# Grouped-query attention: the two heads of a query tile handled as a pair in every step

## The chip, the cores and the metric

One core of a Trainium2 chip. The metric is the device time of one execution in microseconds (us); smaller is better. TensorE is written PE, VectorE DVE, ScalarE ACT, GpSimdE POOL, SyncE SP.

## The reference, cut to what matters

Two different transformer blocks of two layers each, 512 tokens, model width 1024, all in float32. The first block runs four mixers side by side in each of its layers: a Fourier mix, grouped-query attention (GQA), an mLSTM scan and differential attention, then a feed-forward part. The change touches only the GQA, which runs twice, once in each layer of the first block:

```
q = apply_rope(rms_norm(q, g0)); k = apply_rope(rms_norm(k, g1))     # 8 query heads, 2 key heads, 64 wide
sc = einsum('blkgd,bskd->bkgls', q, k) * scale                        # per head 512 x 512
p  = softmax(sc, axis=-1)
y  = einsum('bkgls,bskd->blkgd', p, v)
```

## The kernel before

Activations lie transposed: features on the 128 partitions, 512 tokens along the free axis. Every large product (projections, gates, branch products, feed-forward) goes through one **stream**. One stream step is one call of `next(going)` in `steps` (L497 to L518): three fp32r matmuls of 128x128 by 128x512, high and low halves of weight and input (L508, L509, L510). `advance(n)` issues n steps. Most products are 8 steps long, a branch product is 4 (two of them share a weight unit). Weights come in pieces of 4 steps: SP loads `raw`, ACT rounds it to `wh` (L969), POOL takes the difference `wl` (L2035), in a ring of 4 pieces.

What is not a stream product is woven into the stream by hand. `tensor_program`, `scalar_program` and `vector_program` hold the same loops, and `beat(i, ...)` tells ACT and DVE how many products and pieces PE has issued at that place, so that each engine evicts finished products (DVE, `leave` L1376 and others; `branch_out` L1451), applies tanh or squares (ACT) and splits pieces (`split_weights`, which at a beat waits for the piece that PE finished there, L967 to L969) at the same place in its own order. All engines work strictly in the order written.

**GQA stage** (L679 to L714). A task is one head and one block of 128 queries: 32 tasks, ordered query tile p, head, block j. The two heads of a tile lie on partitions 0 to 63 and 64 to 127. For task t:

- PE `scores` (L566): one float32 matmul, 64 rows deep, 128x512 result, in bank 2, 3 or 4 by t % 3.
- DVE `maximum` (L1583), ACT `soften` (L1113, exponential straight from the bank, with the sum), DVE `normalise` (L1613 reciprocal, L1618 scaling), the latter in step t+1.
- PE `turn_over` (L575): four 128x128 transposes in bank 5 or 6 by t % 2, in step t+3. ACT `keep_turned` (L1131) copies them to `probT`.
- After block 3, in step t+4, PE multiplies with the values (L707): four matmuls 128 deep with 64 columns of weights, each 512 columns wide, out on partitions 0 to 63 of bank 7 for the first head, 64 to 127 for the second. After the second head ACT and DVE split bank 7 into the high and low halves of a branch input (L1000, L1385).

Step t is: scores(t), `advance(2)`, turn_over(t-3), the value products where due, `advance(2)`; n+5 = 37 steps, 148 stream steps. The query tiles 2 and 3 are still being prepared inside the loop: `mean` (L540) and `turn_rope` (L546) on PE, `rstd` on ACT (L975 loads the table of logarithms, L983 Ln, L985 Exp), `normed`, `straight` and `turned` on DVE. Their banks are 6 (tile 2) and 5 (tile 3), the banks of the transposes, and `take(b, ...)` makes PE wait until the last reader of a bank is done.

**The stream during and after the GQA** (`stream1`, L113). Counted in steps from the stage's first score, products end at: gate 8, bq 2 at 16, branch 20 and 24, bq 3 at 32, gates 40 and 48, branch 52 and 56, gates 64 and 72, branch 76 and 80, gates 88 and 96, branch 100 and 104, then cq 112, ck 120, cv 128, co 136, cq 144, gate 152, ck 160, gate 168, cv 176, branch 180 and 184, co (tile 1) 192, cq 200, gate 208, ck 216, gate 224, cv 232, branch 236 and 240, co (tile 2) 248, cq 256, gate 264, ck 272, gate 280, cv 288, branch 292 and 296, co (tile 3) 304, and so on to dq 1 at 360, dk 1 at 368.

**The mLSTM stage** follows (L717 to L764): four heads, each with `turn_values` (L554), four small matmuls (L727, L731) into banks 4 to 7, `advance(6)`, and nine scan steps of `advance(3)`, `advance(2)`, so 51 stream steps a head. At the end of head h ACT copies the four result banks out (`sums_of`, L1218 and L1219), and the next head's L727 waits for it. In the ninth scan step of head h, DVE first evicts what has ended in `advance(3)` and then runs `output_low` (L1385) for head h-1, and `sums_of(h)` waits for that. After the four heads: `advance(4)`, `turn_values`, `finish_of(i, "dk", 1)`, which runs the stream up to the end of dk 1, wherever it stands.

The differential attention later uses the same `scores` with two score matmuls a task, one on partitions 0 to 63 and one on 64 to 127, next to each other in the order.

Of the kernel before, what the change touches and what calls it, by code (L numbers as in the profile page):

```python
# [15 lines left out]
P = 128  # L16
# [236 lines left out]
class Program:  # L253
# [75 lines left out]
    def gqa_tasks(self):  # L329
        out = []  # L330
        for p in range(4):
            for hd in range(2):
                rows = slice(hd * HQ, (hd + 1) * HQ)
                probT = self.w(8, 4) if hd == 0 else self.w(17, 4)
                for j in range(NT):
                    out.append(Task([self.gqa_q(p)[rows, :]], [self.w(23)[rows, :]], j, S, 0, probT, 2 * p + hd,
                                    j == NT - 1, slot=hd))
        return out
# [121 lines left out]
def tensor_program(g):  # L460
# [117 lines left out]
    def layer1(i):  # L578
# [101 lines left out]
        n = len(tasks)  # L680
        probs = [w(4 + r) for r in range(4)]
        for t in range(n + 5):
            if t == 0:
                pe.wait_ge(s_dve, at("V", "rope", i, "k"))
            if t < n:
                if t % 8 == 0:
                    pe.wait_ge(s_dve, at("V", "rope", i, f"q{t // 8}"))
                scores(i, "gqa", tasks, t)
            if t == 1:
                turn_rope(i, chains["q1"])  # L690
            if t in (8, 14):
                mean(i, chains["q2" if t == 8 else "q3"])
            if t in (11, 17):
                turn_rope(i, chains["q2" if t == 11 else "q3"])
            advance(2)
            beat(i, "gqa", t, 0)
            if 0 <= t - 3 < n:
                turn_over(i, "gqa", tasks, t - 3, probs[(t - 3) % 4])
            if 0 <= t - 4 < n and tasks[t - 4].last:
                k = tasks[t - 4]  # L700
                hd = k.slot
                pe.wait_ge(s_act, at("C", "pT", i, "gqa", t - 4))
                if hd == 0:
                    pe.wait_ge(s_dve, at("V", "vt", i, "gqa"))
                    take(7, s_dve, "V", "H", i, 1, k.head // 2)
                for m in range(NT):
                    mm = nc.tensor.matmul(bank[7][hd * HQ:(hd + 1) * HQ, :],  # L707
                                          w(24)[:, m * P + hd * HQ:m * P + (hd + 1) * HQ],
                                          k.probT[:, m * S:(m + 1) * S], start=m == 0, stop=m == NT - 1)
                mm.then_inc(s_pe, T("pv", i, "gqa", k.head))  # L710
            advance(2)
            beat(i, "gqa", t, 1)
# [241 lines left out]
def scalar_program(g):  # L954
# [178 lines left out]
    def layer1(i):  # L1133
# [43 lines left out]
        n = len(tasks)  # L1177
        probs = [[w(4 + r) for r in range(4)]]
        for t in range(n + 5):
            if t < n:  # L1180
                soften(i, "gqa", tasks, t, probs)
            beat(i, "gqa", t, 0)
            if t in (8, 14):
                name = "q2" if t == 8 else "q3"
                rstd(i, name, g.gqa_chain(i, name).bank, g.gqa_chain(i, name).tmp)
            if 0 <= t - 3 < n:
                keep_turned(i, "gqa", tasks, t - 3)
            if 0 <= t - 4 < n and tasks[t - 4].last and tasks[t - 4].slot == 1:
                head = tasks[t - 4].head
                act.wait_ge(s_pe, at("T", "pv", i, "gqa", head))  # L1190
                branch_high(i, 1, head // 2, bank[7][:, :])
            beat(i, "gqa", t, 1)
# [159 lines left out]
def vector_program(g):  # L1352
# [396 lines left out]
    def layer1(i):  # L1749
# [80 lines left out]
        n = len(tasks)  # L1830
        probs = [[w(4 + r) for r in range(4)]]
        for t in range(n + 5):
            if t < n:
                maximum(i, "gqa", tasks, t, probs)
            beat(i, "gqa", t, 0)
            if t in (1, 11, 17):
# [618 lines left out]
```

## Time and profile before

| what | value |
|---|---|
| median of 3 runs | 3653.83 us (3651.8 to 3656.82) |
| profiled execution: its own time | 3656.83 us |
| profiled execution: span, first to last instruction | 3655.5 us |
| mean granted PE clock over the span | 0.981 |
| GQA stage, layer 0 and layer 1 | 192.3 us each |

The profile is of one execution. PE is its matmuls, PEld its weight loads. Matmuls overlap their neighbours in the records, so the price of an instruction is read from start to start, not from its own length. A float32 matmul shows as two records. Idle time before a group, and what ended it, stands in brackets.

### The profile page before, as it was taken

What the parts mean: (1) busy time and instruction counts of PE and PEld (TensorE: products, weight loads), DVE (VectorE), ACT (ScalarE), POOL (GpSimd) and SP (SyncE); (2) the same over time, 40 slices, a digit from 0 to 9 for tenths busy, and PEclk for the clock granted to TensorE, in tenths of its full rate; (3) what the DMA queues carried; (4) which work ended last, traced back from release to release, by engine and by line L of the source; (5) the groups of instructions that cost most, each with busy time, mean ns of one, the idle gap of its engine ahead of it and who ended that gap; (6) DMA issues with size and microseconds to landing.
All of it is one profiled execution on the core that took longest, in us unless ns stands there. A gap on an engine that the chain in (4) does not pass through costs nothing.

```text
span 3655.5 us, 39205 instructions
## 1 busy us (share of the span) xinstructions
PE 3515.7 (96%) x14412; PEld 2601.9 (71%) x14412; DVE 1459.8 (40%) x2796; ACT 1367.3 (37%) x2605; POOL 1320.1 (36%) x1016
## 2 busy tenths in 40 slices
PE   8999999999999999999999989988899999789999
PEld 5556776787787755667677778864588886468887
DVE  3432457444324243255644352355422124542212
ACT  2343334533223244333544322345433234543222
POOL 1222333344444322323244534430144443025444
PEclk9999999999999999999999999998999999899999
DMA  4111112233323211112123322210033322013333
GB/s 159 52 67 55 58 64 65 69 98 122 99 95 96 64 52 47 63 55 70 58 77 111 111 81 94 97 64 24 31 110 104 97 95 81 12 41 104 98 98 104
DMA packets 154751, 286.80 MB, mean 78 GB/s; under 512 B 17980, under 2 KB 20061, under 8 KB 154432
## 3 DMA queue, kind: packets, MB, share of 16 engines
q1 hardware_dynamic: 153232, 281.90, 23.9%
q8 instruction: 115, 1.88, 0.2%
q10 hardware_dynamic: 1328, 2.39, 0.2%
q14 instruction: 76, 0.62, 0.1%
HBM read 278.85 MB, written 5.37 MB: 78 GB/s over the span
## 4 chain that ended last, share of the span: by engine, by line
PE 83%; DVE 9%; ACT 5%; issue 2%; POOL 2%; DMA 0%; ACTq 0%; POOLq 0%; DVEq 0%
PE bank L508 23%; PE bank L510 22%; PE bank L509 22%; PE bank L566 3%; DVE work L1425 2%; POOL wl L2035 2%; PE bank L707 2%; PE bank L625 2%; PE bank L575 1%; ACT wh L969 1%; DVE work L1376 1%; PE bank L742 1%; PE bank L756 1%; PE bank L754 1%; PE bank L933 1%
## 5 line engine op out<-in xcount | busy, mean ns | idle before, releaser
L2035 POOL TENSOR_TENSOR wl<-raw,wh 128x512 fp32r<-128x512 f32 x1012 | 1319.9, 1317 | 2323.7 <-ACT wh L969 2100.0
L508 PE MATMUL bank<-Uh,wh 128*128 128x512 f32 x2720 | 1144.4, 421 | 36.5 <-POOL wl L2035 22.3
L510 PE MATMUL bank<-Uh,wl 128*128 128x512 f32 x2720 | 1068.9, 393 | 0.0
L509 PE MATMUL bank<-Ul,wh 128*128 128x512 f32 x2720 | 1067.5, 392 | 0.0
L969 ACT ACTIVATE wh<-raw 128x512 fp32r<-128x512 f32 x1012 | 601.8, 621 | 641.3 <-PE bank L510 621.3
L508 PEld LDWEIGHTS bank<-Uh,wh 128*128 128x128 f32 x2720 | 515.1, 189 | 255.0 <-issue 117.6
L509 PEld LDWEIGHTS bank<-Ul,wh 128*128 128x128 f32 x2720 | 516.3, 190 | 123.0 <-issue 23.0
L510 PEld LDWEIGHTS bank<-Uh,wl 128*128 128x128 f32 x2720 | 514.6, 189 | 112.0
L1376 DVE TENSOR_TENSOR work<-bank,rs 128x512 f32<-128x512 f32 x308 | 212.8, 691 | 895.1 <-PE bank L510 857.8
L508 PE MATMUL bank<-Hh,wh 128*128 128x512 f32 x1258 | 503.1, 400 | 9.0 <-ACT work L1060 5.9
L510 PE MATMUL bank<-Hh,wl 128*128 128x512 f32 x1258 | 490.4, 390 | 0.0
L509 PE MATMUL bank<-Hl,wh 128*128 128x512 f32 x1258 | 490.1, 390 | 0.0
L508 PEld LDWEIGHTS bank<-Hh,wh 128*128 128x128 f32 x1258 | 236.1, 188 | 84.4 <-issue 12.1
L510 PEld LDWEIGHTS bank<-Hh,wl 128*128 128x128 f32 x1258 | 236.1, 188 | 50.3
L509 PEld LDWEIGHTS bank<-Hl,wh 128*128 128x128 f32 x1258 | 236.4, 188 | 48.3 <-issue 1.9
L1410 DVE TENSOR_TENSOR xT<-xT,bank 128x512 f32<-128x512 f32 x128 | 88.0, 688 | 437.8 <-PE bank L510 437.8
L1075 ACT ACTIVATE work<-work 128x512 f32<-128x512 f32 x88 | 55.7, 633 | 380.6 <-DVE work L1425 245.8
L1081 ACT ACTIVATE Hh<-work 128x512 fp32r<-128x512 f32 x88 | 55.8, 634 | 312.4 <-DVE work L1437 312.4
L566 PE MATMUL bank<-work 64*128 64x512 f32 (+4 forms) x352 | 143.7, 592 | 4.1 <-DVE small L1587 4.1
L1113 ACT ACTIVATE work<-work,small 128x512 f32<-128x512 f32 (+3 forms) x160 | 95.5, 597 | 124.6 <-DVE small L1597 85.0
L1015 ACT ACTIVATE work<-xT 128x512 f32<-128x512 f32 x72 | 45.4, 630 | 204.8 <-DVE xT L1410 188.5
L575 PEld LDWEIGHTS bank<-const,work 128*128 128x128 f32 x588 | 75.0, 143 | 59.4 <-issue 17.8
(206 smaller groups left out, 2841.5 us busy)
## 6 DMA issues: line engine op xcount, KB each, us to landing
raw<-in_units SPq DMA_DIRECT2D x1012, 256.0 KB, 2.8
work<-in_dft SPq DMA_DIRECT2D x6, 512.0 KB, 9.4
xT<-in_xT SPq DMA_DIRECT2D x8, 256.0 KB, 9.2
scratch<-work SPq DMA_DIRECT2D x1, 2048.0 KB, 7.7
out<-xT SPq DMA_DIRECT2D x8, 256.0 KB, 2.9
table<-scratch SPq DMA_DIRECT2D x4, 448.0 KB, 5.1
work<-in_dft SPq DMA_DIRECT2D x2, 640.0 KB, 11.3
scratch<-table SPq DMA_DIRECT2D x1, 1152.0 KB, 5.3
```

The source lines that it names most:

```text
L508: nc.tensor.matmul(out, H, xh, start=k == 0, stop=False)
L509: nc.tensor.matmul(out, H, xl, start=False, stop=False)
L510: mm = nc.tensor.matmul(out, L, xh, start=False, stop=k == x.kt - 1)
L566: nc.tensor.matmul(bank[b][:, 0:k.nk], q[:, k.j * P:(k.j + 1) * P], keys[:, k.key0:k.key0 + k.nk], start=True, stop=True).then_inc(s_pe, T ...
L575: mm = nc.tensor.transpose(bank[b][:, n * P:(n + 1) * P], prob[:, n * P:(n + 1) * P], c("ident"))
L625: mm = nc.tensor.matmul(bank[b][:, :], g.work[:, x:x + P], w(8 + 4 * cs + j), start=j == 0 and cs == 0, stop=j == NT - 1 and cs == 1)
L707: mm = nc.tensor.matmul(bank[7][hd * HQ:(hd + 1) * HQ, :], w(24)[:, m * P + hd * HQ:m * P + (hd + 1) * HQ], k.probT[:, m * S:(m + 1) * S], ...
L969: nc.scalar.activation(g.wh[:, a:a + PK * P], g.raw[:, a:a + PK * P], ACT.Copy).then_inc(s_hi, 1)
L1113: nc.scalar.activation(prob, src, ACT.Exp, bias=mx, accum_out=sm).then_inc(s_act, C("ex", i, st, t, p))
L1376: nc.vector.tensor_tensor(out, b, g.RS, ALU.mult).then_inc(s_dve, V(*key))
L1410: nc.vector.tensor_tensor(k, k, bank[x.bank][:, :], ALU.add).then_inc(s_dve, V("ev", i, x.kind, x.t))
L2035: nc.gpsimd.tensor_tensor(g.wl[:, a:a + PK * P], g.raw[:, a:a + PK * P], g.wh[:, a:a + PK * P].bitcast(F32), ALU.subtract).then_inc(g.s_lo, 1)
```

## The change

`gqa_tasks` now orders the tasks by tile, block, head, so that tasks 2x and 2x+1 are the two heads of one block. The loops of all three engines run over pairs x, n = 16, for n+3 = 19 steps:

- PE issues both score matmuls of pair x next to each other, then `advance(4)`, then (if pair x-2 was the last of its tile) the value products of both heads, eight matmuls whose output alternates between partitions 0 to 63 and 64 to 127, then both transposes of pair x-1, then `advance(4)`. So there are 152 stream steps.
- DVE takes both maxima, evicts up to the middle beat, does `turned` where due, then normalises both tasks of pair x-1. ACT does both exponentials, its middle beat, `rstd` where due, the branch copy, then copies the transposes of pair x-1.
- The means of tiles 2 and 3 stand in steps 4 and 7 (before: 8 and 14 of the single steps), their rotations in steps 5 and 8.

```diff
@@ -327,14 +327,14 @@
                      self.gqa_q(t))
 
     def gqa_tasks(self):
+
         out = []
         for p in range(4):
-            for hd in range(2):
-                rows = slice(hd * HQ, (hd + 1) * HQ)
-                probT = self.w(8, 4) if hd == 0 else self.w(17, 4)
-                for j in range(NT):
-                    out.append(Task([self.gqa_q(p)[rows, :]], [self.w(23)[rows, :]], j, S, 0, probT, 2 * p + hd,
-                                    j == NT - 1, slot=hd))
+            for j in range(NT):
+                for hd in range(2):
+                    rows = slice(hd * HQ, (hd + 1) * HQ)
+                    out.append(Task([self.gqa_q(p)[rows, :]], [self.w(23)[rows, :]], j, S, 0,
+                                    self.w(8, 4) if hd == 0 else self.w(17, 4), 2 * p + hd, j == NT - 1, slot=hd))
         return out
 
     def mlstm_tiles(self, h):
@@ -677,39 +677,41 @@
         beat(i, "F", 15)
 
         tasks = g.gqa_tasks()
-        n = len(tasks)
+        n = len(tasks) // 2
         probs = [w(4 + r) for r in range(4)]
-        for t in range(n + 5):
-            if t == 0:
-                pe.wait_ge(s_dve, at("V", "rope", i, "k"))
-            if t < n:
-                if t % 8 == 0:
-                    pe.wait_ge(s_dve, at("V", "rope", i, f"q{t // 8}"))
-                scores(i, "gqa", tasks, t)
-            if t == 1:
+        for x in range(n + 3):
+            if x < n:
+                if x == 0:
+                    pe.wait_ge(s_dve, at("V", "rope", i, "k"))
+                if x % 4 == 0:
+                    pe.wait_ge(s_dve, at("V", "rope", i, f"q{x // 4}"))
+                for hd in range(2):
+                    scores(i, "gqa", tasks, 2 * x + hd)
+            if x == 1:
                 turn_rope(i, chains["q1"])
-            if t in (8, 14):
-                mean(i, chains["q2" if t == 8 else "q3"])
-            if t in (11, 17):
-                turn_rope(i, chains["q2" if t == 11 else "q3"])
-            advance(2)
-            beat(i, "gqa", t, 0)
-            if 0 <= t - 3 < n:
-                turn_over(i, "gqa", tasks, t - 3, probs[(t - 3) % 4])
-            if 0 <= t - 4 < n and tasks[t - 4].last:
-                k = tasks[t - 4]
-                hd = k.slot
-                pe.wait_ge(s_act, at("C", "pT", i, "gqa", t - 4))
-                if hd == 0:
-                    pe.wait_ge(s_dve, at("V", "vt", i, "gqa"))
-                    take(7, s_dve, "V", "H", i, 1, k.head // 2)
+            if x in (4, 7):
+                mean(i, chains["q2" if x == 4 else "q3"])
+            if x in (5, 8):
+                turn_rope(i, chains["q2" if x == 5 else "q3"])
+            advance(4)
+            beat(i, "gqa", x, 0)
+            if 0 <= x - 2 < n and tasks[2 * (x - 2)].last:
+                pair = tasks[2 * (x - 2):2 * (x - 2) + 2]
+                pe.wait_ge(s_act, at("C", "pT", i, "gqa", 2 * (x - 2) + 1))
+                pe.wait_ge(s_dve, at("V", "vt", i, "gqa"))
+                take(7, s_dve, "V", "H", i, 1, pair[0].head // 2)
                 for m in range(NT):
-                    mm = nc.tensor.matmul(bank[7][hd * HQ:(hd + 1) * HQ, :],
-                                          w(24)[:, m * P + hd * HQ:m * P + (hd + 1) * HQ],
-                                          k.probT[:, m * S:(m + 1) * S], start=m == 0, stop=m == NT - 1)
-                mm.then_inc(s_pe, T("pv", i, "gqa", k.head))
-            advance(2)
-            beat(i, "gqa", t, 1)
+                    for hd, k in enumerate(pair):
+                        mm = nc.tensor.matmul(bank[7][hd * HQ:(hd + 1) * HQ, :],
+                                              w(24)[:, m * P + hd * HQ:m * P + (hd + 1) * HQ],
+                                              k.probT[:, m * S:(m + 1) * S], start=m == 0, stop=m == NT - 1)
+                        if m == NT - 1:
+                            mm.then_inc(s_pe, T("pv", i, "gqa", k.head))
+            if 0 <= x - 1 < n:
+                for t in (2 * (x - 1), 2 * (x - 1) + 1):
+                    turn_over(i, "gqa", tasks, t, probs[t % 4])
+            advance(4)
+            beat(i, "gqa", x, 1)
         finish_of(i, "cv", 0)
         beat(i, "M", 0)
 
@@ -1174,22 +1176,24 @@
         beat(i, "F", 15)
 
         tasks = g.gqa_tasks()
-        n = len(tasks)
+        n = len(tasks) // 2
         probs = [[w(4 + r) for r in range(4)]]
-        for t in range(n + 5):
-            if t < n:
-                soften(i, "gqa", tasks, t, probs)
-            beat(i, "gqa", t, 0)
-            if t in (8, 14):
-                name = "q2" if t == 8 else "q3"
+        for x in range(n + 3):
+            if x < n:
+                for hd in range(2):
+                    soften(i, "gqa", tasks, 2 * x + hd, probs)
+            beat(i, "gqa", x, 0)
+            if x in (4, 7):
+                name = "q2" if x == 4 else "q3"
                 rstd(i, name, g.gqa_chain(i, name).bank, g.gqa_chain(i, name).tmp)
-            if 0 <= t - 3 < n:
-                keep_turned(i, "gqa", tasks, t - 3)
-            if 0 <= t - 4 < n and tasks[t - 4].last and tasks[t - 4].slot == 1:
-                head = tasks[t - 4].head
+            if 0 <= x - 2 < n and tasks[2 * (x - 2)].last:
+                head = tasks[2 * (x - 2)].head + 1
                 act.wait_ge(s_pe, at("T", "pv", i, "gqa", head))
                 branch_high(i, 1, head // 2, bank[7][:, :])
-            beat(i, "gqa", t, 1)
+            if 0 <= x - 1 < n:
+                for t in (2 * (x - 1), 2 * (x - 1) + 1):
+                    keep_turned(i, "gqa", tasks, t)
+            beat(i, "gqa", x, 1)
         beat(i, "M", 0)
 
         def weights_of(h, x):
@@ -1827,23 +1831,25 @@
         beat(i, "F", 15)
 
         tasks = g.gqa_tasks()
-        n = len(tasks)
+        n = len(tasks) // 2
         probs = [[w(4 + r) for r in range(4)]]
-        for t in range(n + 5):
-            if t < n:
-                maximum(i, "gqa", tasks, t, probs)
-            beat(i, "gqa", t, 0)
-            if t in (1, 11, 17):
-                turned(i, chains["q" + {1: "1", 11: "2", 17: "3"}[t]])
-            if 0 <= t - 1 < n:
-                normalise(i, "gqa", tasks, t - 1, probs)
-            if t in (8, 14):
-                name = "q2" if t == 8 else "q3"
+        for x in range(n + 3):
+            if x < n:
+                for hd in range(2):
+                    maximum(i, "gqa", tasks, 2 * x + hd, probs)
+            beat(i, "gqa", x, 0)
+            if x in (1, 5, 8):
+                turned(i, chains["q" + {1: "1", 5: "2", 8: "3"}[x]])
+            if 0 <= x - 1 < n:
+                for t in (2 * (x - 1), 2 * (x - 1) + 1):
+                    normalise(i, "gqa", tasks, t, probs)
+            if x in (4, 7):
+                name = "q2" if x == 4 else "q3"
                 normed(i, chains[name])
                 straight(i, chains[name])
-            if 0 <= t - 4 < n and tasks[t - 4].last and tasks[t - 4].slot == 1:
-                branch_low(i, 1, tasks[t - 4].head // 2, bank[7][:, :])
-            beat(i, "gqa", t, 1)
+            if 0 <= x - 2 < n and tasks[2 * (x - 2)].last:
+                branch_low(i, 1, tasks[2 * (x - 2)].head // 2, bank[7][:, :])
+            beat(i, "gqa", x, 1)
         beat(i, "M", 0)
 
         for h in range(4):
```

## Rows read from the trace of the kernel before

**Rows 1.** The page's busy time, share of the span and instructions of each engine.

```profile
PE 3515.7 (96%) x14412; PEld 2601.9 (71%) x14412; DVE 1459.8 (40%) x2796; ACT 1367.3 (37%) x2605; POOL 1320.1 (36%) x1016
```

**Rows 2.** Windows, the two GQA stages: us, busy by engine, clock, DMA share, GB/s.

```profile
143.30:335.60 192.30, 191.06 (x711) 113.00 (x711) 68.12 (x134) 81.98 (x157) 49.28 (x37) 1.00 0.18 60
1306.70:1499.00 192.30, 191.06 (x711) 112.99 (x711) 68.12 (x134) 81.96 (x156) 49.30 (x37) 1.00 0.16 51
```

**Rows 3.** Timeline of PE, one GQA step: start, length, line, [idle before].

```profile
160.33 0.40 PE L510 MATMUL bank<-Uh,wl 128*128 128x512 f32 x1
160.66 1.12 PE L566 MATMUL bank<-work 64*128 64x512 f32 x2
...
162.05 0.40 PE L509 MATMUL bank<-Hl,wh 128*128 128x512 f32 x1
...
163.21 0.60 PE L575 MATMUL bank<-const,work 128*128 128x128 f32 x4
...
163.87 0.39 PE L509 MATMUL bank<-Hl,wh 128*128 128x512 f32 x1
```

**Rows 4.** Timeline of PE, two scores next to each other in the differential attention.

```profile
620.30 0.39 PE L510 MATMUL bank<-Hh,wl 128*128 128x512 f32 x1
620.62 1.13 PE L566 MATMUL bank<-work 64*128 64x512 f32 x4
...
622.01 0.39 PE L509 MATMUL bank<-Hl,wh 128*128 128x512 f32 x1
```

**Rows 5.** Timeline of PE, value products of one head.

```profile
176.59 0.60 PE L575 MATMUL bank<-const,work 128*128 128x128 f32 x4
177.11 3.65 PE L707 MATMUL bank<-work 128*64 128x512 f32 x8
...
181.03 0.40 PE L509 MATMUL bank<-Ul,wh 128*128 128x512 f32 x1
```

**Rows 6.** Timeline of PE, the step with the mean of tile 2.

```profile
182.27 1.12 PE L566 MATMUL bank<-work 64*128 64x512 f32 x2
...
184.52 0.40 PE L509 MATMUL bank<-Ul,wh 128*128 128x512 f32 x1
...
187.08 0.63 PE L575 MATMUL bank<-const,work 128*128 128x128 f32 x4 [1.24 <-ACT work L983]
```

**Rows 7.** Timeline of DVE: maximum, reciprocal, scaling, eviction of a branch product.

```profile
161.82 0.69 DVE L1583 TENSOR_REDUCE small<-bank 128x1 f32<-128x512 f32 x1 [0.36 <-PE bank L566]
162.43 0.15 DVE L1613 RECIPROCAL small<-small 128x1 f32<-128x1 f32 x1
162.62 0.49 DVE L1618 TENSOR_SCALAR work<-work,small 128x512 f32<-128x512 f32 x1
165.23 0.69 DVE L1451 SCALAR_TENSOR_TENSOR merged<-work,bank 128x512 f32<-128x512 f32 x1 [2.13 <-PE bank L510]
```

**Rows 8.** Timeline of ACT: split of a piece, table load of `rstd`.

```profile
147.50 0.63 ACT L969 ACTIVATE wh<-raw 128x512 fp32r<-128x512 f32 x1 [1.51 <-PE bank L510]
...
184.96 1.28 ACT L975 ACT_TABLE_LOAD   x1
```

**Rows 9.** Timeline of PE, three places where it waited.

```profile
444.95 2.07 PE L727 MATMUL bank<-work,const 64*128 64x512 f32 x2 [2.91 <-ACT work L1219]
...
578.03 1.13 PE L566 MATMUL bank<-work 64*128 64x512 f32 x4 [2.04 <-DVE small L1587]
...
1741.52 1.83 PE L566 MATMUL bank<-work 64*128 64x512 f32 x4 [2.05 <-DVE small L1587]
```

**Rows 10.** Windows, the third mLSTM head of layer 0; columns as in rows 2.

```profile
441.40:502.50 61.10, 58.19 (x216) 41.20 (x215) 30.20 (x36) 20.65 (x40) 17.20 (x13) 0.92 0.17 54
```

**Rows 11.** Waits of PE, whole span: us in total, times, longest.

```profile
PE bank L727 <- ACT work L1219: 7.1, 4, 2.9
```

**Rows 12.** Timeline of ACT at the end of the second mLSTM head.

```profile
440.61 0.63 ACT L1042 ACTIVATE work<-work 128x512 f32<-128x512 f32 x1 [1.55 <-DVE work L1376]
...
443.81 0.60 ACT L1218 ACTIVATE work<-bank 128x512 f32<-128x512 f32 x1 [1.53 <-DVE Hl L1385]
```

## The prediction

> **What bounds the kernel now.** I read the page's busy shares first: PE 96%, the other engines under 41% [rows 1]. Then the windows of the two GQA stages: 192.3 us each, PE busy 191.06, clock 1.00 in both [rows 2]. So in these stages PE does one thing after another at full clock, and whatever PE issues less of comes off the time, if no wait takes its place. Third, PE's timeline, for prices from start to start. Fourth, the timelines of DVE and ACT, for when they can release PE in the new order. Last, PE's waits over the whole span, because the stage gets 152 stream steps in place of 148 and so shifts what comes after it.
>
> **Prices on PE.** A stream matmul costs 0.232 us: 162.05 to 163.21 is five of them [rows 3]. From the last L510 before a score to the L509 after it is 1.72 us, 0.46 of it two ordinary spacings: a score costs 1.26. The differential attention issues two scores side by side on the two row halves: four records in 1.13 us, and 1.71 from L510 to L509 [rows 4]. So a pair costs 1.25, what one costs. Transposes: 163.21 to 163.87 less one spacing, 0.43 a task, 0.11 each [rows 3]. Value products: 176.59 to 181.03 is 4.44, less the 0.66 that a plain transpose group takes to the same place, so 3.78 a head for eight records [rows 5]. A mean or rotation: 182.27 to 184.52 is 2.25, where a score alone takes 1.39 to the same place, so 0.86 [rows 3, 6].
>
> **Part 1, scores in pairs.** Per layer 32 x 1.26 = 40.3 becomes 16 x 1.25 = 20.0: -20.3. The pair has the form of the differential attention's (two row halves, two banks, adjacent in the order), so I take that row whole; the lower bound of the gain is nothing.
>
> **Part 2, value products alternating between column halves.** Before 8 x 3.78 = 30.2 a layer. No row shows two column halves next to each other. If they run together as row halves do, both heads cost one: 4 x 3.78 = 15.1, that is -15.1. If they do not, only some 0.2 a pair is saved. If the alternation even exposes loads and costs a fifth more per record, both heads take about 9.1 in place of 7.6: +6 a layer. I take full overlap, by the nearest row [rows 4]; the others bound the range.
>
> The rows show that eight records in one column half already follow each other at 3.65 / 8 = 0.46 us [rows 5], so their weight loads lie under matmuls. 
>
> **Part 3, transposes and rotations.** Both transpose groups stand together, but each transpose costs 0.11 wherever it stands: 0. Rotations and means: the same number, 0. The four more stream steps are taken from the part up to dk 1, which runs the stream to a fixed product: 0. ACT's copies, now after the transposes in the same step, are read a step later: covered by the `advance(4)` behind them. Weights: a step had 4 stream steps in 4.5 us, now 8 in some 7.7; ACT splits up to four pieces ahead, and one lasts 2.8 us, so its detours in the loop are covered. No DMA is issued at another piece.
>
> **Part 4, the new wait.** Before, a task was normalised two steps ahead of its transposes. Now DVE has from the scores to the middle of the same step. With the scores' start as 0, PE reaches the first transposes at 1.39 + 11 x 0.232 = 3.94 and the second at 4.38. DVE [rows 3, 7]: first maximum at 1.16, the second at 1.77, reciprocal 2.38, scaling 2.57 to 3.06, the second task's 3.25 to 3.74. Plain steps are on time, by 0.8 and 0.6. Steps 1 and 8 add two operations of `turned` (1.34), but also 0.86 of rotation on PE: 4.4 and 5.1 against 4.80 and 5.24, on time. Steps 5, 9, 13 and 17 have value products in between.
>
> Steps 2, 6, 9 and 12 have a branch product that ends exactly at the middle beat (20, 52, 76, 100). DVE must evict it first, 0.11 after PE goes on (165.23 is such an eviction [rows 7]): 4.05, reciprocal 4.66, scaling to 5.34, the second to 6.02. The second transposes start at 6.1 and not 4.38: 1.7 us. In step 9 the value products cover it. So 3 x 1.7 = +5.1 a layer. Behind it on PE wait 4 stream steps and the next scores.
>
> Steps 4 and 7: the bank of the mean is the bank of a transpose, whose `take` waits for Ln. ACT now reaches `rstd` behind the middle beat, at which it splits the piece just finished. PE is at 4.80; the split begins about 0.2 later (an estimate) and takes 0.63, and from the table load to the released transpose are 187.08 - 184.96 = 2.12 [rows 6, 8]: 7.8. In step 4 the second transposes use bank 6, planned for 5.24: 2.5. In step 7 the first use bank 5, planned for 4.80: 3.0. Before, step 8 waited once: 187.08 against 184.52 + 5 x 0.232 = 185.68, 1.4. So +4.1 a layer.
>
> **The clock.** A gap of 2.91 us was followed by records of twice the length (2.07 for two) and a mean clock of 0.92 over 61.1 us: 4.9 us lost, TensorE at 1.2 and not 2.4 GHz for about 10 us [rows 9, 10]. Of the two gaps of 2.04 and 2.05 one left the clock alone (1.13), the other did not (1.83) [rows 9]. Step 7's 3.0 is like the first: +4.9 a layer. Step 4's 2.5 lies between; I count nothing for it and keep up to 4.9 a layer in the range.
>
> **Part 5, the shifted stream.** Before, the second mLSTM head stands at step 250 at its end, its ninth scan step's middle at 248: exactly where co of tile 2 ends. So DVE evicts it, ACT applies its tanh, and only then come `output_low` and `sums_of` [rows 12]; PE waits 2.91 and the clock falls [rows 9]. With four more steps the middle is at 252, co has been evicted half a scan step earlier, and the wait goes: -2.9 - 4.9. At the third head the reverse: its end moves from 301 to 305, and co of tile 3 ends at 304, so its eviction (0.7), tanh and a split (0.6 each) come ahead of `sums_of`. I get 1.9 in place of (7.1 - 2 x 2.9) / 2 = 0.65 [rows 11]: +1.2. Net -6.6 a layer. The wait ahead of the differential attention (2.04 [rows 9]) stays: DVE's chain there starts at dk 1.
>
> **Sum.** Per layer -20.3 - 15.1 + 5.1 + 4.1 + 4.9 - 6.6 = -27.9; two layers -56. The profiled execution took 3656.8 us (span 3655.5 and 1.3 around it), 3.0 over the median of the three runs. So 3601 like for like, and 3598 for the median.
>
> **Rivals.**
> *A: the column halves do not run together* (also what the skill's rule on weight loads says). Nothing in the trace shows that they do. Price 2 x 15.1 less 8 x 0.2: 3598 + 29 = 3627; with exposed loads 3598 + 2 x 21 = 3640. Chance 0.20.
> *B: slower; the middle of every step waits for DVE.* Where? At the transposes (L575) for `scaled`. For it: slack is only 0.6, and DVE's work of a pair now lies in 4 us. Against: DVE's chain in a plain step is five short rows, on time. To bring the time above that of before it must eat 56 us over the 8 plain steps of each layer, 3.5 in each, or have the clock fall in some: five gaps of 3.0 with their slow stretches (7.9 each) in each layer give 3598 + 79 = 3677. It decides from four such gaps a layer. Chance 0.05.
> *C: the scores of a pair don't overlap*, because something between them (the bank of the second waits for the exponential of two tasks ago) parts them. That exponential is done a step earlier. 3598 + 40 = 3638. Chance 0.04.
> *D: neither gap of Part 4 lowers the clock and branch steps wait less.* 3598 - 10 - 10 = 3578. Chance 0.10, at the range's edge.
>
> **Numbers.** My forecast, 3598, holds with 0.61 within some 12 us. The range 3578 to 3638 takes in D, A at its plain price with step 4's clock falls, and C. A measurement of this kernel can tell a change from none at about 0.2%, 7 us. Faster by more: forecast, A, C, D and most of what is between, 0.92. Slower by more: B, 0.05. Within: 0.03.
>
> **What would show it.** Scores: records of L566 in fours within 1.13 us, 1.71 from L510 to L509. Value products: 16 records of L707 in about 3.6 us (A: 7.2). Steps 2, 6, 12: a gap of 1.5 ahead of a transpose; steps 4 and 7: gaps of about 2.4 and 2.9 put down to L983, the latter followed by a clock of 0.5. The GQA stage should last some 192.3 + 2.8 - 35.4 + 9.2 + 4.9 = 174 us. At the third mLSTM head no wait of 2.9, at the fourth one of about 1.9. The prediction is wrong if the value records keep their spacing, if gaps stand in plain steps, or if other mLSTM waits appear.

## The result, and the profile after

| | time | what |
|---|---|---|
| before | 3654.07 us | median of 5 (3651.8 to 3656.82) |
| changed | 3633.46 us | median of 5 (3620.98 to 3636.89) |
| ratio | 0.9938 | 95% interval 0.9919 to 0.9956 |

The change makes the kernel faster, by 21 us. I had forecast 3598, a gain of 56. The time lies in the range, near its upper end, but the gain is less than half of what I had forecast.

The five executions of the changed kernel lie 16 us apart, those of before 5. The profiled one is the fastest of the five. Below, the busy shares of the page of the changed kernel, which answer to [rows 1]:

```profile
PE 3452.0 (95%) x14412; PEld 2593.0 (72%) x14412; DVE 1467.5 (41%) x2796; ACT 1358.8 (38%) x2605; POOL 1317.6 (36%) x1016
```

Windows of the changed kernel: the GQA stage and the mLSTM stage of layer 0 and of layer 1. Columns as in rows 2, the last but two being the granted clock:

```profile
138.66:321.20 182.54, 167.48 (x723) 114.00 (x723) 71.28 (x134) 78.77 (x157) 48.82 (x38) 0.95 0.20 65
1284.67:1465.75 181.08, 166.03 (x723) 112.48 (x723) 71.31 (x134) 78.55 (x157) 48.82 (x38) 0.96 0.17 55
321.20:556.07 234.87, 229.26 (x937) 169.74 (x935) 120.00 (x144) 83.59 (x158) 77.68 (x57) 1.00 0.20 65
1465.75:1707.08 241.33, 235.73 (x937) 173.12 (x935) 120.13 (x144) 83.60 (x158) 77.71 (x57) 0.97 0.20 63
```

The GQA stages took 192.3 us with PE busy for 191.06 and a clock of 1.00 [rows 2]. Now they take 182.5 and 181.1, and PE is busy for 167.5 and 166.0: 15 us of idle time each where there was 1.2, and a clock of 0.95 and 0.96. I had expected 174.

PE's timeline of the changed kernel shows both pairings in full. A pair of scores, as in [rows 4], and all value products of a tile, where [rows 5] shows one head alone:

```profile
168.06 0.39 PE L510 MATMUL bank<-Hh,wl 128*128 128x512 f32 x1
168.38 1.13 PE L566 MATMUL bank<-work 64*128 64x512 f32 x4
...
169.77 0.39 PE L509 MATMUL bank<-Ul,wh 128*128 128x512 f32 x1
...
193.55 3.66 PE L705 MATMUL bank<-work 128*64 128x512 f32 x16
197.14 1.09 PE L575 MATMUL bank<-const,work 128*128 128x128 f32 x8
```

Four score records in 1.13 us and 1.71 from L510 to L509, as predicted; sixteen value records in 3.66 us, where eight took 3.65. Windows of 0.43 us over the value products (changed kernel, records that touch each window):

```profile
193.53:193.96 0.43, 0.41 (x2) 0.20 (x4) 1.00 0.86 314
193.96:194.39 0.43, 0.43 (x4) 0.14 (x2) 1.00 0.28 91
194.39:194.82 0.43, 0.43 (x4) 0.14 (x2) 1.00 0.00 0
```

One record of either head is under way at a time: a window holds two or four records, where the experiment e_values_apart below shows one or two as long as a single head is at work. So the terms of parts 1 and 2, 35.4 us a layer, came as forecast. What took them back stands in PE's waits of the GQA stage of layer 0 (us in total, times, longest; layer 1 shows the same three lines):

```profile
PE bank L575 <- DVE work L1622: 7.4, 3, 2.5
PE bank L575 <- ACT work L985: 5.3, 2, 2.9
PE bank L546 <- ACT work L1115: 2.3, 1, 2.3
```

Six gaps, 15.0 us. Five of their places in PE's timeline (changed kernel, layer 0; the sixth, at 267.89 in step 12, is again 2.47):

```profile
148.87 1.29 PE L546 MATMUL bank<-merged,const 128*128 128x512 f32 x2 [2.35 <-ACT work L1115]
...
164.44 1.25 PE L575 MATMUL bank<-const,work 128*128 128x128 f32 x8 [2.47 <-DVE work L1622]
...
183.81 1.09 PE L575 MATMUL bank<-const,work 128*128 128x128 f32 x4 [2.43 <-ACT work L985]
...
207.49 1.84 PE L575 MATMUL bank<-const,work 128*128 128x128 f32 x8 [2.47 <-DVE work L1622]
208.98 0.78 PE L508 MATMUL bank<-Hh,wh 128*128 128x512 f32 x1
209.55 0.63 PE L509 MATMUL bank<-Hl,wh 128*128 128x512 f32 x1
...
220.66 1.33 PE L575 MATMUL bank<-const,work 128*128 128x128 f32 x8 [2.87 <-ACT work L985]
```

The gaps of 2.43 and 2.87 (steps 4 and 7) are those that I forecast at about 2.4 and 2.9. Those of 2.47 (steps 2, 6 and 12) I forecast at 1.5. That of 2.35 in step 1 I had not seen. Behind five of the six gaps the ordinary matmuls take 0.63 and not 0.39 us: the clock has fallen. Behind the gap of step 2 (164.44) it has not. Windows of the changed kernel behind three of the gaps:

```profile
149.50:153.50 4.00, 4.00 (x12) 2.85 (x11) 2.50 (x6) 0.00 (x0) 0.00 (x0) 0.57 0.18 66
184.00:188.00 4.00, 4.00 (x14) 3.32 (x14) 1.44 (x2) 2.69 (x4) 0.00 (x0) 0.60 0.19 66
207.90:211.70 3.80, 3.80 (x15) 3.29 (x14) 0.12 (x1) 1.19 (x2) 0.00 (x0) 0.58 0.19 69
```

A mean of 0.57 to 0.60 over 4 us is the level of 1.2 GHz for most of the stretch and 2.4 for the rest; before the gaps it was 1.00. The first window lost 4.00 x 0.43 = 1.7 us. Added up over windows of 1 us, each of the five falls in layer 0 lost 1.7 us, and so did each of four in layer 1 (behind the gaps of steps 2, 4, 6 and 7, not behind those of 1 and 12): nine falls for twelve gaps, 15.4 us. I had priced one fall at 4.9.

**Why 2.47 and not 1.5.** DVE and POOL in step 2, two timelines of the changed kernel. First DVE:

```profile
162.01 0.69 DVE L1455 SCALAR_TENSOR_TENSOR merged<-work,bank 128x512 f32<-128x512 f32 x1 [1.68 <-PE bank L510]
162.61 0.16 DVE L1617 RECIPROCAL small<-small 128x1 f32<-128x1 f32 x1
162.81 1.58 DVE L1622 TENSOR_SCALAR work<-work,small 128x512 f32<-128x512 f32 x1
```

and POOL:

```profile
162.84 1.26 POOL L2041 TENSOR_TENSOR wl<-raw,wh 128x512 fp32r<-128x512 f32 x1 [1.53 <-ACT wh L971]
```

The scaling took 1.58 us where it takes 0.49 [rows 7]. It begins together with POOL's subtraction for the weight piece that was also finished at the middle beat, and ends 0.29 after it. Two more such meetings end alike: a scaling of 1.12 us in e_norm_first ends 0.29 after POOL's subtraction, one of 1.15 in e_both 0.28 after it. The Trainium skill ("SBUF — State Buffer", section "SBUF: two separate sides") says that the port pair which VectorE (in its 2-port modes or with two SBUF inputs) and GpSimd share is an exclusive lock for the whole instruction. The trace fits this, as the scaling is through only when the subtraction is; which mode the scaling runs in, no run shows.

### The profile page after: what moved, and what is told of

The parts are those of the page before. It is cut to its first block, busy times and chain, and to the rows that moved or that the text cites. A ratio compares the mean times of both kernels' runs of the same rounds, so it can differ in the third digit from the quotient of the medians.

```text
span 3619.7 us, 39187 instructions
## 1 busy us (share of the span) xinstructions
PE 3452.0 (95%) x14412; PEld 2593.0 (72%) x14412; DVE 1467.5 (41%) x2796; ACT 1358.8 (38%) x2605; POOL 1317.6 (36%) x1016
## 4 chain that ended last, share of the span: by engine, by line
PE 81%; DVE 9%; ACT 5%; issue 2%; POOL 2%; DMA 0%; ACTq 0%; POOLq 0%; DVEq 0%
PE bank L508 23%; PE bank L510 22%; PE bank L509 22%; PE bank L566 2%; DVE work L1429 2%; POOL wl L2041 2%; PE bank L625 2%; PE bank L575 1%; ACT wh L971 1%; DVE work L1380 1%; PE bank L744 1%; PE bank L758 1%; PE bank L756 1%; PE bank L705 1%; ACT work L1115 1%
## 5 line engine op out<-in xcount | busy, mean ns | idle before, releaser
L510 PE MATMUL bank<-Uh,wl 128*128 128x512 f32 x2720 | 1070.5, 394 | 0.0
L509 PE MATMUL bank<-Ul,wh 128*128 128x512 f32 x2720 | 1068.7, 393 | 0.0
L509 PEld LDWEIGHTS bank<-Ul,wh 128*128 128x128 f32 x2720 | 517.2, 190 | 125.2 <-issue 23.1
L510 PEld LDWEIGHTS bank<-Uh,wl 128*128 128x128 f32 x2720 | 515.5, 190 | 112.3
L510 PE MATMUL bank<-Hh,wl 128*128 128x512 f32 x1258 | 492.4, 391 | 0.0
L509 PE MATMUL bank<-Hl,wh 128*128 128x512 f32 x1258 | 492.3, 391 | 0.0
L510 PEld LDWEIGHTS bank<-Hh,wl 128*128 128x128 f32 x1258 | 237.7, 189 | 50.7
L509 PEld LDWEIGHTS bank<-Hl,wh 128*128 128x128 f32 x1258 | 237.7, 189 | 49.7 <-issue 1.9
L1083 ACT ACTIVATE Hh<-work 128x512 fp32r<-128x512 f32 x88 | 55.8, 634 | 312.4 <-DVE work L1441 312.4
L575 PE MATMUL bank<-const,work 128*128 128x128 f32 x588 | 97.7, 285 | 31.4 <-DVE work L1622 14.8
```

The source lines that it names most:

```text
L509: nc.tensor.matmul(out, H, xl, start=False, stop=False)
L510: mm = nc.tensor.matmul(out, L, xh, start=False, stop=k == x.kt - 1)
L575: mm = nc.tensor.transpose(bank[b][:, n * P:(n + 1) * P], prob[:, n * P:(n + 1) * P], c("ident"))
```

## The experiments

The measure that made the medians readable is the time that an execution cannot have lost to the clock: its time less span x (1 - mean clock). From the span of the profile it is 3619.7 - 76.8 = 3542.9 for the changed kernel and 3655.5 - 70 = 3585 for the one before. From the times of the changed kernel's runs it is 3620.98 - 76 = 3545 and 3636.89 - 91 = 3546. The mean clocks carry three decimals, so each such figure is good to about 2 us. So at full clock the change is worth 43 us, and the clock takes back 7 us in the profile and 18 to 21 in the other four runs. All experiments change `after` and were run with it unless another base is named.

| kernel | median | ratio to before (95%) | clocks of its runs | median less the clock's share |
|---|---|---|---|---|
| before (beside e_both) | 3657.5 | | 0.980 to 0.981 | 3588 |
| after | 3633.5 | 0.9938 (0.9919 to 0.9956) | 0.975 to 0.979 | 3543 |
| after_again | 3635.6 | 0.9943 (0.9931 to 0.9956) | 0.974 to 0.977 | 3545 |
| e_values_apart | 3642.2 | 0.9964 (0.9950 to 0.9977) | 0.976 to 0.979 | 3559 |
| e_scores_apart | 3663.0 | 1.0023 (1.0012 to 1.0033) | 0.978 to 0.979 | 3586 |
| e_bank7 | 3608.7 | 0.9876 (0.9862 to 0.9889) | 0.979 to 0.981 | 3538 |
| e_norm_first | 3607.5 | 0.9858 (0.9843 to 0.9873) | 0.977 to 0.980 | 3532 |
| e_both | 3577.4 | 0.9781 (0.9768 to 0.9794) | 0.982 to 0.984 | 3517 |
| e_short | 3628.9 | 0.9927 (0.9915 to 0.9939) | 0.974 to 0.977 | 3542 |
| e_all | 3580.2 | 0.9788 (0.9775 to 0.9802) | 0.980 to 0.981 | 3510 |
| f_values_parted | 3616.6 | 0.9895 (0.9882 to 0.9909) | 0.980 to 0.981 | 3548 |
| f_scores_apart | 3624.7 | 0.9916 (0.9902 to 0.9929) | 0.980 to 0.982 | 3554 |
| f_one_gap | 3590.8 | 0.9827 (0.9814 to 0.9841) | 0.980 to 0.981 | 3519 |
| f_sums_early | 3566.2 | 0.9757 (0.9743 to 0.9770) | 0.985 to 0.986 | 3513 |

**after_again.** The changed kernel unchanged.

> The changed kernel once more, as the reference for the others. Five runs of it took 3621 to 3637 us, with mean granted clocks from 0.979 (the fastest) to 0.975. Theory G (gaps and clock: the two pairings give their full 35 us a layer, and what is missing went into gaps of 2.4 to 2.9 us in the GQA stage, each followed by a stretch at 1.2 GHz whose length differs between executions): the times scatter by 10 us or more and follow span x (1 - clock). Theory H (a pairing gives less than its records show, the clock is a side effect): the scatter has nothing to do with the clock.

3627 us at a clock of 0.977, 3633 to 3637 at 0.974 and 0.975. In both sets of runs the slower executions are those with the lower clock, and the remainder is 3543 and 3545. So the time does follow the clock, as G has it. But the traces do not show that the scatter comes from the gaps: the traced execution here has falls behind the same nine gaps, of 1.7 us each, as the traced one of 3621 us. The 6.9 us that it lost more to the clock lie at the start of the kernel. Windows of the changed kernel and of after_again:

```profile
36.00:51.00 15.00, 14.83 (x56) 10.35 (x57) 5.73 (x12) 3.10 (x5) 2.50 (x2) 1.00 0.45 148
36.00:51.00 15.00, 15.00 (x29) 8.30 (x30) 3.94 (x7) 1.83 (x3) 1.26 (x1) 0.54 0.18 62
```

That stretch lies ahead of the GQA. None of the slowest executions, those at 0.974 and 0.975, has a trace.

**e_values_apart.**

```diff
-                for m in range(NT):
-                    for hd, k in enumerate(pair):
+                for hd, k in enumerate(pair):
+                    for m in range(NT):
```

> The value products of the first head all before those of the second, everything else as in the changed kernel. G: the 16 records take 7.2 us in place of 3.66, eight times: +28 us over the changed kernel, less what the longer cover gives in the step with a branch product (nothing, it was covered already). H: clearly less than 28, since the overlap would be partly an effect of how the records are drawn.

Seven us by the medians, 16 without the clock's share: neither 28. PE's timeline of this kernel:

```profile
196.91 5.42 PE L705 MATMUL bank<-work 128*64 128x512 f32 x16
```

and windows of 0.43 us in it:

```profile
196.89:197.32 0.43, 0.41 (x1) 0.19 (x2) 1.00 0.94 357
197.75:198.18 0.43, 0.43 (x2) 0.14 (x1) 1.00 0.00 0
199.47:199.90 0.43, 0.43 (x4) 0.19 (x2) 1.00 0.00 0
```

The 16 records take 5.42 and not 7.2 us. At the beginning one or two records touch a window, in the middle four: when the second column half's products stand directly behind the first's, they start before the first's are through. So the experiment took away only half of what it was meant to. 8 x (5.42 - 3.66) = 14, which fits the 16. The expectation was a miss, and f_values_parted was made for it.

**e_scores_apart.**

```diff
                 for hd in range(2):
-                    scores(i, "gqa", tasks, 2 * x + hd)
+                scores(i, "gqa", tasks, 2 * x)
+            advance(1)
+            if x < n:
+                scores(i, "gqa", tasks, 2 * x + 1)
...
-            advance(4)
+            advance(3)
```

> One stream step between the two scores of a pair, the next group of stream steps shorter by one. G: each of the 32 pairs costs 1.25 us more, +40 us over the changed kernel; the gaps in steps 2, 6 and 12 stay, those in 4 and 7 shrink by at most 0.5 since the middle of the step comes later for PE and ACT alike. H: less than 40.

By the medians 27 us, without the clock's share 41. By the medians that is H's result, not G's; f_scores_apart was made to decide. With this pairing undone the kernel is no faster than before. The median clock of its runs is higher than the changed kernel's, though its gaps are nearly the same (1.6 in place of 2.35 in step 1), which is why the medians show less; why it is higher stays open.

**e_bank7.**

```diff
-... "mean64", (3, 2, 6, 5)[t], "rot64" ...
+... "mean64", (3, 7, 7, 7)[t], "rot64" ...
-        rstd(i, "q1", 2, g.gqa_chain(i, "q1").tmp)
+        rstd(i, "q1", 7, g.gqa_chain(i, "q1").tmp)
```

> Means and rotations of query tiles 1, 2 and 3 in bank 7, which is free in those steps, in place of banks 2, 6 and 5. G: the gap of 2.35 us ahead of the rotation in step 1, the 2.43 in step 4 and the 2.87 in step 7 go, in both layers, with their clock falls: 2 x 7.65 = 15 us of gaps and 2 x 3 falls of at least 1.7 us each, 25 us or more less than the changed kernel. H: 15 us, with no change of the mean clock.

27 us under after_again by the medians, as G has it; the clock rose. The three gaps are gone, but two of 0.97 and 0.84 appeared, now on DVE. In both layers together these waits fell by 11.7 us, the time without the clock's share by 5 to 7 only; the rest of it was not found. PE's timeline of e_bank7, the five that are left in layer 0:

```profile
164.58 1.97 PE L575 MATMUL bank<-const,work 128*128 128x128 f32 x8 [2.47 <-DVE work L1622]
...
204.70 1.71 PE L575 MATMUL bank<-const,work 128*128 128x128 f32 x8 [2.47 <-DVE work L1622]
...
224.59 0.66 PE L575 MATMUL bank<-const,work 128*128 128x128 f32 x4 [0.97 <-DVE work L1622]
226.09 0.66 PE L575 MATMUL bank<-const,work 128*128 128x128 f32 x4 [0.84 <-DVE work L1622]
...
262.75 1.71 PE L575 MATMUL bank<-const,work 128*128 128x128 f32 x8 [2.47 <-DVE work L1622]
```

**e_norm_first.** On DVE:

```diff
                 maximum(...)
+            if 0 <= x - 1 < n:
+                ... normalise(i, "gqa", tasks, t, probs)
             beat(i, "gqa", x, 0)
             if x in (1, 5, 8):
                 turned(...)
-            if 0 <= x - 1 < n:
-                ... normalise(i, "gqa", tasks, t, probs)
```

> On DVE the two normalisations of a step come ahead of the middle beat, so that no branch product's eviction stands before them. G: the gaps of 2.47 us in steps 2, 6 and 12 go: 6 x 2.47 = 15 us and six clock falls of 1.7 us or more, 25 us or more less than the changed kernel; the scaling takes 0.5 us and not 1.58, since it no longer falls together with POOL's subtraction of the piece finished at the middle beat. H: 15 us and the same clock.

26 us by the medians: the gaps behind `scaled` are gone, the other three stand in the timeline unchanged (2.35, 2.43, 2.87). The part about the scaling was only half right: it still meets POOL in some steps (1.12 us in step 1 of this kernel), but half a step ahead of the transposes, where it costs nothing.

**e_both.** Both edits.

> Both: bank 7 for the means and rotations, and the normalisations ahead of the middle beat. G: no gap over 1 us is left in the GQA stage; each stage takes 192.3 + 2.8 - 35.4 - 1.4 = 158 us (182.5 and 181.1 in the changed kernel's profile), so 46 us or more less than that profile, near 3573, and a median 50 to 60 us under the changed kernel's 3633. H: 30 us less.

Window of the GQA stage of layer 0, and all of PE's waits in it:

```profile
141.74:301.06 159.32, 158.34 (x724) 108.41 (x724) 70.72 (x134) 77.84 (x157) 50.49 (x38) 1.00 0.22 74
```

```profile
PE bank L705 <- DVE work L1568: 1.0, 1, 1.0
```

159.3 us against 158 expected, PE busy throughout, clock 1.00. The kernel takes 3577 us, 56 under the changed kernel and 80 under the one before: more than the 30 us of gaps alone, so theory H falls. Without the clock's share it is 26 us, near the 28 by which the waits fell (30.1 to 2.0 over both layers); the other 30 are clock. The profiled executions show no fall in the GQA stages any more (15.4 us less).

**e_short.**

```diff
-            advance(4)
+            if x < n + 2:
+                advance(4)
             beat(i, "gqa", x, 1)
         finish_of(i, "cv", 0)
```

> The last group of four stream steps of the GQA loop left out, so that the mLSTM stage again starts 148 steps after the first score. If the shift of the stream is what moved the waits there (the prediction's part 5), the third head's wait is 2.9 us again and the fourth's 0.65, in place of 1.68 and 1.89; the sum of the two is nearly the same, so the time is the changed kernel's within 5 us, up to 10 us more if the clock falls after 2.9 and not after 1.7. If something else moved them, they stay 1.68 and 1.89.

PE's waits over the span, e_short and then the changed kernel:

```profile
PE bank L730 <- ACT work L1224: 7.1, 4, 2.9
```

```profile
PE bank L729 <- ACT work L1223: 7.1, 4, 1.9
```

The wait of 2.9 is back, with the same total of 7.1 as in [rows 11]. Four stream steps do move these waits. The time did not rise: it is 5 to 7 us under the changed kernel's, which is within its scatter.

**e_all.** e_both, with `output_high` and `output_low` ahead of the beat in the ninth scan step.

> e_both, and in the mLSTM stage the high and low halves of the head before are made ahead of the ninth scan step's first beat on ACT and DVE. G: the third head's wait (1.68) goes, as its chain was piece split, high half, low half (1.42 us, beside POOL's subtraction), copy; 2 x 1.7 us and in some executions a clock fall of 3.4 us each under e_both, so 3 to 10 us. The fourth head's 1.89 stays, since its chain is tanh of the fourth o tile.

The third head's wait fell from 1.67 to 0.18 us. Without the clock's share that is 7 us, but the clock was lower (0.980 and 0.981 against 0.982 to 0.984) and the median is 3 us higher than e_both's; the intervals of the two ratios overlap. The 3 to 10 us expected did not show. In the traces the clock lost 5.1 us behind the wait of 1.89 in each layer, and 3.4 in e_both.

**f_values_parted.** On e_both: the first head's value products ahead of the transposes, the second's behind them and two stream steps, ACT's branch copy behind its copies of the transposes.

> On e_both, the kernel without gaps in the GQA stage (3577 us). The second head's value products stand behind the transposes and two stream steps, so that the two column halves are not next to each other at all. When only the alternation was given up (e_values_apart), the 16 records still took 5.42 us and not 7.2. G: that was an overlap of the two halves at their border; apart, each head's 8 records take 3.6 us, and the kernel needs 8 x 3.6 = 29 us more than e_both, near 3606. H: the column halves' records overlap only on paper; the difference is that of e_values_apart, 7 us.

39 us over e_both; without the clock's share 31, 8 x 3.6 = 29 expected. Here 8 records take 3.62 us and the other 8 take 3.65. So 29 to 31 us is what the column halves are worth at full clock; the other 8 us of the medians are clock.

**f_scores_apart.** On e_both, the edit of e_scores_apart.

> On e_both, one stream step between the two scores of a pair. In the changed kernel this cost 27 us by the medians, with fewer microseconds lost to the clock (77 against 91). G: with hardly any clock falls in the stage the whole price shows, 32 x 1.25 = 40 us over e_both, near 3617. H: 27 again, near 3604.

47 us over e_both, 37 without the clock's share, 40 expected: G and not H.

**f_one_gap.** On e_both (and `rstd(i, "q1", 2, ...)` as in the changed kernel):

```diff
-... "mean64", (3, 7, 7, 7)[t], "rot64" ...
+... "mean64", (3, 2, 7, 7)[t], "rot64" ...
```

> e_both with the mean and rotation of query tile 1 back in bank 2, which brings back one gap of about 2.35 us in each layer (step 1) and nothing else. It measures what one such gap costs with its clock fall. G: 2 x 2.35 = 4.7 us of gap and 2 x 1.7 to 2 x 5.1 of clock: 8 to 15 us over e_both. H: 5 us.

13.5 us, for 4.7 us of gap. PE's timeline of f_one_gap and the window behind it:

```profile
151.15 1.10 PE L546 MATMUL bank<-merged,const 128*128 128x512 f32 x2 [2.35 <-ACT work L1115]
```

```profile
150.00:156.00 6.00, 4.85 (x13) 3.54 (x14) 3.25 (x7) 1.01 (x4) 1.06 (x1) 0.72 0.13 44
```

By the medians a gap of 2.35 us thus costs nearly three times its length. The trace accounts for less: one fall behind each of the two gaps, 6.00 x 0.28 = 1.7 us here and 1.7 in layer 1, which makes 8 us with the gaps, where the two profiled executions (3589.0 and e_both's 3579.6) lie 9.4 apart. The median clocks, 0.980 and 0.983, leave more to the clock in the other runs; where, no trace shows.

**f_sums_early.** e_all, and on ACT (the calls of `sums_of` at the heads' borders are taken out):

```diff
+                if x == 8:
+                    sums_of(h)
                 beat(i, "scan", h, x, 1)
```

> e_all, and ACT copies the four result banks of a mLSTM head out ahead of the last beat, before tanh and splits. G: the waits at the heads' borders (4.1 us in all in e_all, of them 2 x 1.9) go to about 1 us. On a full clock 3 us less than e_all, and without the gaps of 1.9 no clock fall there, so 3 to 10 us less: 3570 to 3577. Since e_all gave no gain over e_both in spite of 3 us less waiting, the clock may eat this too; then 3577 to 3580.

3566 us, below the range given: 11 us under e_both and 90 under the kernel before (3655.8 beside it), ratio 0.9757 (0.9743 to 0.9770). The waits of L729 are down to 0.4 us in all. Against e_both 6.7 us of waiting were removed; the clock (0.985) gave the rest: its trace has no fall in the mLSTM stages, that of e_both one of 3.4 us in each. It is the fastest version.

## Why the prediction was right or wrong

**Right.** Parts 1 and 2, the prices and their mechanism: 1.25 us a pair of scores (f_scores_apart: 37 us for 40), both heads' value products for the price of one (f_values_parted: 31 for 29). Rivals A and C did not come true: the 16 records took 3.66 us, and the four score records 1.13. The rule of the Trainium skill ("TensorE: Matmul & The Clock Gate", Part 3, The mechanism), that a weight load overlaps a matmul in flight only when the row group differs, does not hold for these two column halves: they share all rows, and the gain was 7.2 / 3.66, near two. Part 3 held, but for the bank of one rotation (below). The waits for Ln in steps 4 and 7 came as priced, 2.43 and 2.87.

**Wrong, gaps.** At full clock I had -55.8 us, measured -43. Three terms of the sum were missed or mis-sized, for both layers:
- Step 1, "on time": 2 x 2.35 = 4.7. I counted no wait there, since I followed DVE and not PE's bank. The rotation of tile 1 goes to bank 2, and with pairs the second score of step 1 has just been written there, so the rotation must wait for the exponential of task 3. I had checked this for banks 6 and 5 and not for 2.
- Part 4, the branch steps: 2.6 us late and not 1.7, 6 x 0.9 = 5.5, since the scaling ran into POOL's subtraction. Both follow the same event, the piece finished at the middle beat. My price was that of an undisturbed scaling.
- Part 5: I had the third head's wait go; it fell from 2.91 to 1.68, 2 x 1.68 = 3.4. The eviction of co is out of the way, as forecast, but a piece now ends at the middle of the ninth scan step, its split stands ahead of `output_high`, and `output_low` takes 1.42 us. e_all removed it by putting them ahead of the beat. The fourth head's 1.9 was right.

Together 13.6, against 13 measured.

**Wrong, clock.** I counted one fall of 4.9 us a layer (step 7) and one saved (the mLSTM's), net 0. The step that failed is "Step 4's 2.5 lies between; I count nothing for it", and with it the price, which was taken from one fall. In the profiled execution the clock fell behind nine of the twelve gaps and lost 1.7 us each time: 15.4 us where the sum had 9.8. And the mLSTM's falls did not go with its wait of 2.91: they lost 10.2 us before and 6.8 after, behind the waits of 1.68 and 1.89 in layer 1, so 3.4 was saved and not 9.8. Windows of the kernel before, then of the changed one:

```profile
444.00:455.00 11.00, 10.05 (x15) 4.86 (x16) 1.98 (x3) 1.88 (x4) 0.00 (x0) 0.53 0.07 24
1608.00:1619.00 11.00, 10.68 (x17) 5.39 (x18) 1.79 (x3) 1.88 (x4) 0.10 (x1) 0.53 0.04 14
1576.00:1584.00 8.00, 8.00 (x19) 4.91 (x18) 2.61 (x5) 0.63 (x1) 1.28 (x1) 0.57 0.00 0
1634.00:1642.00 8.00, 8.00 (x17) 4.55 (x16) 4.13 (x7) 0.41 (x1) 0.00 (x0) 0.57 0.07 27
```

That makes +12 against my net 0. Falls elsewhere, where the two programs do the same, happened to lose 5 us less, hence the +7 of the profile. In the median the clock takes back 21, and 13 + 21 = 34 of the 35 us by which it misses 3598; where the other 14 us of clock lie has no trace.

**Luck.** The time lies inside the range, but not for the reasons that drew it: the upper end, 3638, stands for rivals A and C, which did not come true. Of what happened the range held only the falls behind step 4's gap.

**Rival B** had the right danger and the wrong place: plain steps showed no wait, the slower side stayed far.

What stays open: why a gap of about 2 us costs a clock fall in one place or execution and none in another. The same gaps of 1.68 and 1.89 left the clock alone in layer 0 and not in layer 1 (windows: 1.00 and 0.97). Open too is which part of the scatter between executions comes from the gaps.

## What to carry to other kernels

When tasks are paired, check every wait of the new order in each engine and for each bank, the helpers' banks too; here two cheap edits turned a gain of 21 us into 80, and two more into 90. Count a fall of the clock behind a PE gap of 2.35 us or more unless a trace shows none: nine of twelve had one here, of 1.7 us each, and by the medians e_both gained 56 us for 28 us of waits. And judge variants by their time without the clock's share beside the median. Work that becomes due at the same event on two engines which slow each other, as DVE's scaling and POOL's subtraction do, must be priced together.

## What the runs showed of the hardware

- Float32 matmuls 128 deep with 64 columns of weights run two at a time when they alternate between column halves: 16 records in 3.66 us against 3.62 and 3.65 for 8. Without alternation, but adjacent, 16 take 5.42: they overlap at the border, where I expected none.
- A DVE scaling from SBUF to SBUF of 0.49 us took 1.58 beside a POOL subtraction of 1.26, and 1.15 and 1.12 where it began 0.43 us into one. In all three cases it ended 0.28 to 0.29 us after the subtraction.
- Behind nine of twelve PE gaps of 2.35 to 2.87 us the granted clock fell to 1.2 GHz and the fall lost 1.7 us; behind the same waits of 1.68 and 1.89 us it fell in one layer and not in the other.
- A gap of 2.35 us in each of two places cost 13.5 us by the medians (e_both and f_one_gap), of which traces show 8. Executions of the changed kernel differ by up to 16 us and their mean clocks by 0.004; those of e_both, without gaps in the GQA stage, by 3.5 us (3576 to 3580).
